# Attention scores of blocks 1 to 3: one 32-bit product in place of three rounded ones

## What is computed

```
qb = q.reshape(b, nb, BLOCK, N_KV_HEADS, Q_PER_KV, HEAD_DIM)
k_band = jnp.concatenate([prev(kb), kb], axis=2)
s_band = jnp.einsum('bnqkgd,bnskd->bnkgqs', qb, k_band).astype(jnp.float32) * scale
s_meta = jnp.einsum('bnqkgd,bmkd->bnkgqm', qb, meta_k).astype(jnp.float32) * scale
s_band = jnp.where(band_mask[None, :, None, None], s_band, NEG_INF)
probs = softmax_with_sink(jnp.concatenate([s_band, s_meta], axis=-1), sinks)
out = einsum(probs[..., :2 * BLOCK], v_band) + einsum(probs[..., 2 * BLOCK:], meta_v)
```

## Time and profile before

| | us |
|---|---|
| median of 3 runs | 1236.63 |
| lowest and highest run | 1234.3 and 1239.9 |
| span of the profiled execution | 1234.6 |
| prompt's attention, blocks 1 to 3 | about 418 to 541 |
| expert loop | about 822 to 1180 |

### The profile page before, as it was taken

One profiled execution on the slowest core, in us unless ns is written; L12 is line 12 of the kernel. 1 busy time (PEld: TensorE's weight loads), 2 busy tenths in 40 slices (PEclk: granted clock), 3 DMA queues, 4 the chain that ended last, 5 costly groups with the idle time before them and its releaser, 6 DMA issues. The chain is left out here.

```text
span 1234.6 us, 12489 instructions
## 1 busy us (share of the span) xinstructions
PE 1057.8 (86%) x4433; PEld 736.4 (60%) x4433; DVE 484.4 (39%) x1073; ACT 305.6 (25%) x721; POOL 165.2 (13%) x132
## 2 busy tenths in 40 slices
PE   6999993887896999999899999439999999999910
PEld 6998893666674778778788444414444444444400
DVE  6774298476835333350354133511111111111157
ACT  5333311224533322241431110101111111111120
POOL 0001263454003201000000011020000000000043
PEclk9999987788895555557999999669999999999955
DMA  7322216922355000010511300349998989989641
GB/s 259 92 97 59 69 35 244 421 88 73 123 170 217 31 6 1 1 68 1 221 69 69 137 1 1 136 173 320 349 338 330 331 329 341 344 332 327 225 156 68
DMA packets 37277, 205.33 MB, mean 166 GB/s; under 512 B 8117, under 2 KB 8597, under 8 KB 27169
## 3 DMA queue, kind: packets, MB, share of 16 engines
q1 hardware_dynamic: 30944, 182.18, 40.6%
q0 software_dynamic: 3984, 14.17, 3.2%
q10 hardware_dynamic: 2304, 8.39, 1.7%
HBM read 166.87 MB, written 37.76 MB: 166 GB/s over the span
## 5 line engine op out<-in xcount | busy, mean ns | idle before, releaser
L818 PE MATMUL bank<-w_f,x_f 128*128 128x512 f32 x512 | 226.6, 596 | 1.0 <-DVE x_f L1627 1.0
L818 PEld LDWEIGHTS bank<-w_f,x_f 128*128 128x128 f32 x512 | 96.6, 191 | 116.6 <-issue 116.6
L485 PE MATMUL bank<-r_r,w_r 128*128 128x268 f32 (+1 forms) x464 | 152.4, 329 | 14.9 <-DVE w_r L1170 10.1
L487 PE MATMUL bank<-r_r,w_r 128*128 128x268 f32 x416 | 121.0, 291 | 0.0
L486 PE MATMUL bank<-y_r,w_r 128*128 128x268 f32 x416 | 120.8, 290 | 0.0
L826 PE MATMUL bank<-w_f,x_f 128*128 128x512 f32 x256 | 115.1, 592 | 0.0
L485 PE MATMUL bank<-x_r,r_r 128*128 128x512 f32 x240 | 100.0, 417 | 14.1 <-DVE w_r L1430 8.8
L485 PEld LDWEIGHTS bank<-r_r,w_r 128*128 128x128 f32 (+1 forms) x464 | 94.9, 205 | 20.6 <-DVE w_r L1170 10.1
L486 PE MATMUL bank<-w_r,r_r 128*128 128x512 f32 x240 | 98.2, 409 | 0.0
L487 PE MATMUL bank<-x_r,w_r 128*128 128x512 f32 x240 | 97.8, 408 | 0.0
L1638 DVE SCALAR_TENSOR_TENSOR x_f<-bank,y_f,x_f 128x256 f32<-128x256 f32 x32 | 15.5, 484 | 202.7 <-ACT x_f L1131 202.7
(11 more groups left out here) (315 smaller groups left out, 1624.4 us busy)
## 6 DMA issues: line engine op xcount, KB each, us to landing
w_f<-in_w_gu SPq DMA_DIRECT2D x32, 2048.0 KB, 8.7
w_f<-in_w_d SPq DMA_DIRECT2D x32, 1024.0 KB, 8.0
w_f<-in_w_f SPq DMA_DIRECT2D x26, 512.0 KB, 3.5
scr_x<-y_f SPq DMA_DIRECT2D x1, 12800.0 KB, 45.7
w_f<-in_w_t SPq DMA_DIRECT2D x6, 2048.0 KB, 8.1
x_f<-scr_x SPq DMA_DIRECT2D x17, 512.0 KB, 9.5
scr_y<-x_f ACTq DMA_DIRECT2D x16, 512.0 KB, 9.1
scr_y<-y_f SPq DMA_DIRECT2D x1, 4096.0 KB, 55.2
```

The source lines that it names most:

```text
L485: pe.matmul(out, ah, bh, start=start, stop=False)
L487: return pe.matmul(out, al, bh, start=False, stop=stop)
L818: ins = pe.matmul(pb[2 + u][:, :], XT[:, k, :], wgu[u][:, k, :], start=(k == 0), stop=(k == KC - 1))
```

## The change

The score of blocks 1 to 3 becomes two 32-bit products straight from `qT` and `kd`: one of the 16 meta columns, and one of the 256 columns of the block before and the own block, which are neighbours in `kd`. The latter writes two runs of 128 columns, 144 apart, so that the bank keeps its order. The wait for `kx_pl` before a score goes, and with it POOL's rounded copies and differences and their tiles (`kx`, `kl`, `qh`, `ql`). Apart from that, the separate semaphores of the softplus steps and of the samples' attention are merged into one for each engine that raises them (`sp_dv`, `sa_dv`, `sa_mm`, `sa_ac`), with the waits' counts raised accordingly.

```diff
                 if b == 0:
                     ins = pe.matmul(out[:, P:AW], q, key[:, SEQ0:PR0 + P], start=True, stop=True)
                 else:
-                    pe.wait_ge(S["kx_pl"], 2 * b + 1)
-                    ins = split_product(pe, out[:, 0:AW], qh[b - 1][r0:r0 + HD, h // 2, :],
-                                        ql[r0:r0 + HD, h // 2, PR0 + P * b:PR0 + P * (b + 1)],
-                                        kx[b - 1][r0:r0 + HD, g, :], kl[b - 1][r0:r0 + HD, g, :], True, True)
+                    pe.matmul(out[:, P:P + NMETA], q, key[:, SEQ0:PR0], start=True, stop=True)
+                    both = out[:, 0:2 * (P + NMETA)].rearrange("p (a s) -> p a s", a=2)[:, :, 0:P]
+                    ins = pe.matmul(both, q, key[:, PR0 + P * (b - 1):PR0 + P * (b + 1)], start=True, stop=True)
                 ins.then_inc(S["s_mm"], 1)
...
                  .then_inc(S["pm_pl"], 1)
-                b = i // KVH + 1
-                if b < NBLK and i % KVH < 2:
-                    (pool_block_high, pool_block_low)[i % KVH](p, b)
...
-            pe.wait_ge(S["spn_dv"], 1)
+            pe.wait_ge(S["sa_dv"], 4)
```

More of the change, by code:

```diff
@@ L178, in build @@
         A1 = R1 + 12 * AW + 768 + 2 * P
[L179 to L182, removed]
         pM = [cut(R1 + 9920 + 64 * i, QPK * NMETA) for i in range(2)]
@@ L190, in build @@
         Vm = cut(RX + 6656, NSAMP, KVH * HD)
-        kx = [cut(R1 + 5632 + KVH * AW * b, KVH, AW, whole=rounded) for b in range(NBLK - 1)]
         A2 = R1 + 3264
@@ L407, in sp_gates @@
             sp_gate_weights(sp, 4)
-            sp.wait_ge(S["spv_mm"], 1)
+            sp.wait_ge(S["sa_mm"], 4)
             sp.dma_start(wo_a, io["w_o"][:, 0:KC // 2, :]).then_inc(S["wo_in"], 16)
@@ L417, in sp_residual @@
         def sp_residual(sp):
-            sp.wait_ge(S["sot_mm"], 1)
-            sp.wait_ge(S["spn_dv"], 1)
+            sp.wait_ge(S["sa_mm"], 5)
+            sp.wait_ge(S["sa_dv"], 4)
             sp.wait_ge(S["o_dv"], NBLK)
@@ L517, in pe_decays @@
         def pe_decays(pe):
-            pe.wait_ge(S["sp3_dv"], 1)
+            pe.wait_ge(S["sp_dv"], 2)
             for t in range(1, NT + 1):
@@ L530, in pe_ssd @@
             pe.wait_ge(S["f_ev"], FT)
-            pe.wait_ge(S["sp4_dv"], 1)
+            pe.wait_ge(S["sp_dv"], 3)
             pe.wait_ge(S["bf_dv"], 1)
@@ L677, in pe_sample_attention @@
         def pe_sample_attention(pe):
-            pe.wait_ge(S["qs_dv"], 1)
+            pe.wait_ge(S["sa_dv"], 1)
             pe.wait_ge(S["cache_in"], 16 * (2 * NSAMP + 3))
@@ L687, in pe_sample_attention @@
                     ins = pe.matmul(pb[1][0:NMETA, c], Km[:, n, pair, :], q, start=True, stop=True)
-            ins.then_inc(S["ss_mm"], 1)
-            pe.wait_ge(S["ss_ev"], 1)
+            ins.then_inc(S["sa_mm"], 1)
+            pe.wait_ge(S["sa_dv"], 2)
             pe.transpose(pb[2][:, 0:P], sT[:, 0:P], ident)
-            pe.transpose(pb[2][:, P:P + NMETA], sTm[0:NMETA, 0:P], ident[0:NMETA, 0:NMETA]).then_inc(S["st2_mm"], 1)
+            pe.transpose(pb[2][:, P:P + NMETA], sTm[0:NMETA, 0:P], ident[0:NMETA, 0:NMETA]).then_inc(S["sa_mm"], 1)
             pe_gates(pe, N_Z, N_Z + 1)
-            pe.wait_ge(S["spn_dv"], 1)
+            pe.wait_ge(S["sa_dv"], 4)
             pe.transpose(pb[0][:, 0:P], s2[:, 0:P], ident)
-            pe.transpose(pb[0][0:NMETA, P:2 * P], s2[:, P:P + NMETA], ident).then_inc(S["pt2_mm"], 1)
+            pe.transpose(pb[0][0:NMETA, P:2 * P], s2[:, P:P + NMETA], ident).then_inc(S["sa_mm"], 1)
             pe_gates(pe, N_Z + 1, N_Z + 2)
-            pe.wait_ge(S["pt2_ev"], 1)
+            pe.wait_ge(S["sa_ac"], 2)
             pe.wait_ge(S["cache_in"], 16 * (2 * NSAMP + 3))
@@ L703, in pe_sample_attention @@
                     ins = group(pe, pb[1][:, c], [(Vs[:, n, v], pTs[:, c]), (Vm[0:NMETA, n, v], pTm[0:NMETA, c])])
-            ins.then_inc(S["spv_mm"], 1)
+            ins.then_inc(S["sa_mm"], 1)
             pe_gates(pe, N_Z + 2, N_Z + 3)
-            pe.wait_ge(S["so_ev"], 1)
+            pe.wait_ge(S["sa_ac"], 3)
             for h in range(H):
@@ L709, in pe_sample_attention @@
                                    ident[0:HD, 0:HD])
-            ins.then_inc(S["sot_mm"], 1)
+            ins.then_inc(S["sa_mm"], 1)
         def pe_gates(pe, first, last):
@@ L730, in pe_mix @@
         def pe_mix(pe):
-            pe.wait_ge(S["sya_dv"], 1)
+            pe.wait_ge(S["sa_dv"], 5)
             pe.wait_ge(S["c_ac"], 6 * NT)
@@ L917, in act_softplus @@
             link = act_link[0]
-            act.wait_ge(S["sp1_dv"], 1)
+            act.wait_ge(S["sp_dv"], 1)
             link(act.activation(dex[:, :, :], dab[:, :, :], ACT.Exp, scale=-1.0))
@@ L1009, in act_sample_attention @@
         def act_sample_attention(act):
-            act.wait_ge(S["qs_dv"], 1)
+            act.wait_ge(S["sa_dv"], 1)
             act.wait_ge(S["small_out"], 80)
@@ L1013, in act_sample_attention @@
             act_high(act, 1)
-            act.wait_ge(S["sx_dv"], 1)
+            act.wait_ge(S["sa_dv"], 3)
             act.activation(s2[:, 0:P + NMETA], s2[:, 0:P + NMETA], ACT.Exp, bias=scol[:, 1:2], accum_out=scol[:, 2:3])
-            act.activation(scol[:, 3:4], pk("sink_col"), ACT.Exp, bias=scol[:, 1:2]).then_inc(S["sp_ac"], 1)
+            act.activation(scol[:, 3:4], pk("sink_col"), ACT.Exp, bias=scol[:, 1:2]).then_inc(S["sa_ac"], 1)
             act_gate(act, N_Z)
-            act.wait_ge(S["pt2_mm"], 1)
+            act.wait_ge(S["sa_mm"], 3)
             act.copy(pTs[:, 0:P], pb[0][:, 0:P])
-            act.copy(pTm[0:NMETA, 0:P], pb[0][0:NMETA, P:2 * P]).then_inc(S["pt2_ev"], 1)
+            act.copy(pTm[0:NMETA, 0:P], pb[0][0:NMETA, P:2 * P]).then_inc(S["sa_ac"], 1)
             act_gate(act, N_Z + 1)
-            act.wait_ge(S["spv_mm"], 1)
+            act.wait_ge(S["sa_mm"], 4)
             for p in range(2):
@@ L1257, in dve_chunk_decays @@
             v.tensor_tensor(tmc[0:NMETA, META, :], tot[0:NMETA, META, :], ncs[0:NMETA, META, :], ALU.add)
-            v.tensor_tensor(tmc[:, 1:NT, :], tot[:, 1:NT, :], ncs[:, 1:NT, :], ALU.add).then_inc(S["sp4_dv"], 1)
+            v.tensor_tensor(tmc[:, 1:NT, :], tot[:, 1:NT, :], ncs[:, 1:NT, :], ALU.add).then_inc(S["sp_dv"], 1)
         def dve_decay_rows(v, c, g):
@@ L1268, in dve_ssd @@
             link = dve_link[0]
-            v.wait_ge(S["sp3_dv"], 1)
+            v.wait_ge(S["sp_dv"], 2)
             for g in range(KVH):
@@ L1399, in dve_sample_attention @@
                     ins = v.tensor_copy(Ks[half, :, pair, NWK], kd[half, 2 * pair + p, 0:NSAMP])
-            ins.then_inc(S["qs_dv"], 1)
+            ins.then_inc(S["sa_dv"], 1)
             dve_low(v, 1)
-            v.wait_ge(S["ss_mm"], 1)
+            v.wait_ge(S["sa_mm"], 1)
             v.tensor_copy(sT[:, 0:P], pb[0][:, 0:P])
-            v.tensor_copy(sTm[0:NMETA, 0:P], pb[1][0:NMETA, 0:P]).then_inc(S["ss_ev"], 1)
-            v.wait_ge(S["st2_mm"], 1)
+            v.tensor_copy(sTm[0:NMETA, 0:P], pb[1][0:NMETA, 0:P]).then_inc(S["sa_dv"], 1)
+            v.wait_ge(S["sa_mm"], 2)
             link(v.tensor_scalar(s2[:, 0:P + NMETA], pb[2][:, 0:P + NMETA], SCALE, None, ALU.mult))
@@ L1413, in dve_sample_attention @@
             v.tensor_scalar(s2[:, 0:P + NMETA], s2[:, 0:P + NMETA], scol[:, 5:6], None, ALU.mult)\
-             .then_inc(S["spn_dv"], 1)
-            v.wait_ge(S["sot_mm"], 1)
+             .then_inc(S["sa_dv"], 1)
+            v.wait_ge(S["sa_mm"], 5)
             for k in range(2):
                 ins = v.tensor_copy(YA[0:NSAMP, 0, 512 * k:512 * (k + 1)], pb[2 + k][0:NSAMP, :])
-            ins.then_inc(S["sya_dv"], 1)
+            ins.then_inc(S["sa_dv"], 1)
         def dve_low(v, part):
@@ L1451, in dve_gates @@
         def dve_gates(v):
-            v.wait_ge(S["sya_dv"], 1)
+            v.wait_ge(S["sa_dv"], 5)
             v.wait_ge(S["o_dv"], NBLK)
```

33 lines of the change are left out of this document (9 added, 24 removed).

## The result

The changed kernel takes 1266.61 us (median of four runs, 1265.41 to 1267.69); the kernel before took 1236.95 beside it. The ratio is 1.0233, with a 95% interval from 1.0213 to 1.0253: slower by 29.7 us. The forecast was 1265.4.

What follows compares the result with a forecast made beforehand. PE, full at half clock in attention blocks 1 to 3, was taken as the bound. 48 x 0.60 = 28.8 us on the 1234.6 us span gave 1263.4, plus 2.0 to the median: 1265.4 us, range 1256 to 1271.

Steps and rivals of the forecast that it cites:

- What bounds the kernel: Blocks 1 to 3 of the prompt's attention: PE busy 42.00 of 44 us at clock 0.50, every score on the path.
- The score, 1.57 us: Each score of blocks 1 to 3: 0.17 + 0.43 + 0.85 + 0.12 = 1.57 us, against 0.97 before.
- 48 times 0.60, 28.8 us: Three blocks of 16 heads: 48 scores, each 0.60 us longer on PE, 28.8 us slower in all.
- Nothing from POOL, the wait and the semaphores: Removed rounding on POOL, PE's removed wait for POOL before each score, and merged semaphores: each taken as worth nothing.
- Nothing given back behind the attention: From 541 us on, no waiting DMA issue hides a delay; a shift of the attention's end shifts the whole.
- Shorter loads: Rival: weight loads run at their own pace, the 16-column product adds 0.21, score 1.35 us, total 1255; chance 0.10.
- The clock: Rival: PE's clock rises to full in blocks 1 to 3, heads take 1.47 us, 42 us less, 1195; chance 0.04.
- The split output: Rival: writing 256 columns in two runs costs up to 0.43 us a score, 21 us more, 1286; chance 0.06.
- An absorbed delay: Rival: a transfer between 541 and 822 us hides the shift, up to all of it, 1237; chance 0.02.

## Why the prediction was right, step by step

**What bounds the kernel.** PE, full and at half clock. Shown: DVE's wait for PE grew by the 28.8 us of the sum, POOL's load made no difference, and what halves PE's time on the scores shortens the kernel.

**The score, 1.57 us.** Met, and its terms one by one. The 16-column product was taken at 0.43 between bounds of 0.05 and 0.55: 0.42, by leaving it out. The forecast had the short product's own two loads in this term; by the starts above they are its second and the wide product's first, of the same size. The rest, 0.17 for the first load, 0.85 for two records of 256 columns and 0.12 to the transpose, was 1.14: 1.15. The order of the two products, which the forecast took as it stood, decides 0.18 of the 0.42.

**48 times 0.60, 28.8 us.** 28.9 by the maximum's starts, 28.8 by DVE's waits.

**Nothing from POOL, the wait and the semaphores.** For POOL's work and the semaphores shown together, by the kernel that keeps both: 1266.75 against 1266.61. For the wait no run alone shows it. No line of the list behind the earlier trace rows has PE waiting for POOL, and the kernel with one product of 272 columns has such a wait and a score of 1.20 us, as worked out without it.

**Nothing given back behind the attention.** 289.2 us to the experts before, 289.4 after.

**The rivals.** *Shorter loads* would have made the score 1.35; it fell with the loads without a stream over them, 0.22 and 0.21 us each. *The clock* stayed at 0.50 in blocks 1 to 3 in every kernel here. *The split output* fell by the kernel that joins it. *An absorbed delay* fell by the experts' start.

The total came out 1.2 us above the forecast, less than the three runs of the kernel before differ among themselves.

## What to carry to other kernels

On an engine that is full, count an edit by its records, what each streams and which loads stand uncovered, not by its columns alone: 16 columns of 272 cost 0.42 of a 1.57 us score. If a short product can't be avoided, put it behind a long one, whose stream hides a load. And where a product uses 64 of the 128 rows, look first whether a neighbour can run on the other 64: that gave 2.6% here, more than the change cost.

## What the hardware showed

Matmuls on the two halves of the rows overlap fully even when three of the one half are issued ahead of three of the other (0.98 us for six, 0.97 for three); the expectations had left this open. And, as forecast, PE, though busy 96% of the time (51.67 of 54 us after), stayed at a granted clock of 0.50 through the attention, in the changed kernel and in all eight kernels of the experiments. A load with no stream over it took 0.21 to 0.22 us there, and its place decides whether that counts: 16 columns cost 0.42 us ahead of 256 and 0.24 behind them.
